# A two-block network on one core: two first units of a stage on the un-normed residual, the reciprocal norm on their result, and attention's first unit tile by tile

## The chip, the core and the metric

The kernel runs on one core of a Trainium2 chip. The metric is the device time of one execution in microseconds (us). Five engines run their own instruction streams and meet at semaphores: TensorE (PE, matmuls; PEld is its weight load), VectorE (DVE), ScalarE (ACT), GpSimd (POOL) and SyncE (SP), which starts the DMA transfers.

## The reference, cut to what matters

Two blocks of two layers work on `x`, 256 tokens by 1024 channels, in float32. Every layer is a feed-forward network, a mixer and a second network, and each of these stages begins with an RMS norm over the channels. In the first block:

```python
def rms_norm(x, g):
    xf = xf * lax.rsqrt(jnp.mean(xf * xf, axis=-1, keepdims=True) + NORM_EPS)
    return (xf * g).astype(x.dtype)

def swiglu_ffn(h, w_gu, w_down):
    gate, up = jnp.split(h @ w_gu, 2, axis=-1)
    return (jax.nn.silu(gate) * up) @ w_down

for layer in range(DEPTH):
    h = rms_norm(x, ffn1_norm[layer])
    x = x + 0.5 * swiglu_ffn(h, ffn1_w_gu[layer], ffn1_w_down[layer])
    h = rms_norm(x, mix_norm[layer])
    p = h @ w_in            # gates, an SGU branch, and a part that is shifted by one token
    ...                     # chunked SGU, RWKV-7 recurrence, projections
    x = x + merged @ w_out[layer]
    h = rms_norm(x, ffn2_norm[layer])
    x = x + 0.5 * swiglu_ffn(h, ffn2_w_gu[layer], ffn2_w_down[layer])
return rms_norm(x, final_norm)
```

In the second block the mixers are two attentions, and each norm is followed by a modulation with rows made from a condition vector: `h = rms_norm_2(x, g) * (1 + scale) + shift`, and the result of a stage enters `x` through a gate.

## The kernel before

**Layout.** Channels lie on the partitions: `x` is 8 tiles of 128 channels by 256 tokens, and so is the normed input `h_split`. Every product keeps float32 accuracy by splitting both operands into a rounded part and the rest and adding three matmuls (`three`, L1793 to L1795; `tokens_major` and the attention's helper have their own three, L2257 to L2259). Weights come from memory as 1 MB units of 16 tiles in three `raw_units` slots. A unit is two halves of 8 tiles. ACT writes the rounded part of a half (L852), DVE the rest (L1212), into four `split_halves` slots, and PE uses a pair of halves for one unit of two output tiles: 48 matmuls of 256 columns. Both engines are kept at most three halves ahead of PE by calls of `keep_ahead(w)` that stand at fixed places of their streams; a half can only be split when the slot's last user, four halves earlier, has been multiplied. Results go to three rotating PSUM banks, `linear_banks`.

**A network** (`ffn`) is 22 units for gate and up, each followed by SiLU on ACT (L915), the product on DVE (L1297) and the split of the result, and then a down stage of four pairs of output tiles (d = 0 to 3), each added to `x` by `residual` (L1316, L1323). During the networks DVE also works through the modulation matrix in dot products (L1278).

**A norm** (numbered 0 to 12 in program order; 6 closes the first block and 7 to 12 belong to the second) is a chain over three engines. ACT squares `x` two tiles at a time, PE sums the squares with a constant matrix in two float32 matmuls a pair (L1856, four records in the trace), ACT takes the root (L878) and DVE the reciprocal (L1227). Squares and sums of the pairs 0 to 2 are done in the stage before, as `x` becomes final; pair 3 can only follow the last residual. Then, in five steps (one tile, one tile, and three times two tiles), DVE multiplies `x` by gain and reciprocal (L1265, L1267), ACT rounds (L897; with the shift added L902) and DVE makes the rest (L1244; L1249 with shift). PE's first unit after a norm takes the tiles as they come (`h_wait`), its two halves turn by turn for each tile. In attention PE first waits for all eight tiles, then starts; the first unit of attention 0 has only 16 columns a matmul (the forget gates).

**What follows in the recurrent mixer** (`rwkv`): 13 units whose result ACT copies out of PSUM (L939, `raw_shift`), after which DVE forms the difference to the previous token (L1338) and mixes (L1347).

The order of all of this is written out by hand, engine by engine; `make_plan` only counts the uses of banks and halves.

## Time and profile before

| | |
|---|---|
| three runs, median | 3055.59 us (3054.66 to 3061.22) |
| the profiled execution, its own time | 3053.73 us |
| its span in the trace | 3052.0 us |
| PE busy | 2869.9 us, 94% |
| DVE busy | 1949.7 us, 64% |
| ACT busy | 1440.9 us, 47% |
| mean granted PE clock | 0.967 |

The profile lists each engine's busy time, the granted TensorE clock, the chain of work that ended last, and groups of instructions with what ended the idle time before them. Some 1.7 us lie outside the span. Matmuls overlap one another, so the number of matmuls started in a stretch says more than PE's busy share in it.

### The profile page before, as it was taken

The page shows a single profiled execution, that of the slowest core. Times are in us where ns is not written, and L with a number is a line of the kernel's source. Part 1 is how long each engine was busy: PE and PEld are TensorE (multiplying, and loading weights), DVE is VectorE, ACT ScalarE, POOL GpSimd, SP SyncE. Part 2 cuts the span into 40 slices and gives each one's busy share as a digit, 9 for nine tenths or more (in the row PEclk, how much of TensorE's full clock was granted, in tenths as well). Part 3 has the DMA queues.
Part 4 walks back from the last instruction along what each step waited for, and adds up shares of the span by engine and source line. Part 5 has one row for each costly group of instructions (what it writes and reads, how often), then busy time and mean ns, then how long its engine had stood idle before and what let it go on. Part 6 is the DMA issues. An engine that isn't in the chain of part 4 may idle for free.

```text
span 3052.0 us, 60529 instructions
## 1 busy us (share of the span) xinstructions
PE 2869.9 (94%) x26460; PEld 2738.7 (90%) x26460; DVE 1949.7 (64%) x2828; ACT 1440.9 (47%) x2121; POOL 13.2 (0%) x23
## 2 busy tenths in 40 slices
PE   7999989989999999899899899897999998998899
PEld 7999777889999997778899899886999998998899
DVE  5667556666666676566666666565666666776554
ACT  4445534344444445344344444464444445766443
POOL 0000000000000000000000000000000000000000
PEclk9999999999999999899999999898999999999899
DMA  6665311236656743111456566432665663342354
GB/s 228 238 247 180 111 43 43 84 138 235 248 196 252 264 161 118 50 44 43 166 192 234 182 236 243 161 125 83 239 244 196 252 250 131 133 150 100 129 188 140
DMA packets 72792, 511.09 MB, mean 167 GB/s; under 512 B 8464, under 2 KB 9104, under 8 KB 11728
## 3 DMA queue, kind: packets, MB, share of 16 engines
q1 hardware_dynamic: 72528, 507.21, 46.1%
q8 instruction: 209, 3.42, 0.4%
q14 instruction: 55, 0.45, 0.0%
HBM read 506.13 MB, written 1.05 MB: 166 GB/s over the span
## 4 chain that ended last, share of the span: by engine, by line
PE 89%; DVE 5%; ACT 4%; issue 1%; DMA 0%; SPq 0%; DVEq 0%; ACTq 0%
PE linear_banks L1793 22%; PE linear_banks L1794 21%; PE linear_banks L1795 21%; PE linear_banks L2257 3%; PE linear_banks L2258 3%; PE linear_banks L2259 3%; PE solve_banks L2123 1%; PE linear_banks L2089 1%; PE solve_banks L1856 1%; PE solve_banks L2132 1%; PE solve_banks L2220 1%; DVE rstd L1227 1%; PE solve_banks L2306 1%; PE solve_banks L2287 1%; PE solve_banks L2209 1%
## 5 line engine op out<-in xcount | busy, mean ns | idle before, releaser
L1212 DVE TENSOR_TENSOR split_halves<-raw_units,split_halves 128x1024 fp32r<-128x1024 f32 x806 | 981.5, 1223 | 580.4 <-ACT split_halves L852 578.5
L852 ACT ACTIVATE split_halves<-raw_units 128x1024 fp32r<-128x1024 f32 x806 | 846.3, 1056 | 672.6 <-PE linear_banks L1795 590.4
L1793 PE MATMUL linear_banks<-h_split,split_halves 128*128 128x256 f32 x3744 | 1088.0, 291 | 48.9 <-DVE h_split L1244 27.5
L1794 PE MATMUL linear_banks<-h_split,split_halves 128*128 128x256 f32 x3744 | 1071.5, 286 | 0.0
L1795 PE MATMUL linear_banks<-h_split,split_halves 128*128 128x256 f32 x3744 | 1070.9, 286 | 0.0
L1793 PEld LDWEIGHTS linear_banks<-h_split,split_halves 128*128 128x128 f32 x3744 | 730.6, 195 | 65.0 <-issue 50.5
L1794 PEld LDWEIGHTS linear_banks<-h_split,split_halves 128*128 128x128 f32 x3744 | 731.4, 195 | 2.0 <-issue 1.9
L1795 PEld LDWEIGHTS linear_banks<-h_split,split_halves 128*128 128x128 f32 x3744 | 730.8, 195 | 0.0
L1793 PE MATMUL linear_banks<-hidden_split,split_halves 128*128 128x256 f32 x1408 | 397.4, 282 | 0.0
L1795 PE MATMUL linear_banks<-hidden_split,split_halves 128*128 128x256 f32 x1408 | 394.7, 280 | 0.0
L1794 PE MATMUL linear_banks<-hidden_split,split_halves 128*128 128x256 f32 x1408 | 394.7, 280 | 0.0
L1794 PEld LDWEIGHTS linear_banks<-hidden_split,split_halves 128*128 128x128 f32 x1408 | 265.6, 189 | 0.4
L1793 PEld LDWEIGHTS linear_banks<-hidden_split,split_halves 128*128 128x128 f32 x1408 | 265.6, 189 | 0.4
L1795 PEld LDWEIGHTS linear_banks<-hidden_split,split_halves 128*128 128x128 f32 x1408 | 265.6, 189 | 0.0
L2257 PE MATMUL linear_banks<-split_halves,h_split 128*128 128x256 f32 (+1 forms) x784 | 229.8, 293 | 21.7 <-DVE h_split L1249 21.7
L2258 PE MATMUL linear_banks<-split_halves,h_split 128*128 128x256 f32 (+1 forms) x784 | 225.2, 287 | 0.0
L2259 PE MATMUL linear_banks<-split_halves,h_split 128*128 128x256 f32 (+1 forms) x784 | 224.9, 287 | 0.0
L915 ACT ACTIVATE silu<-linear_banks 128x256 f32<-128x256 f32 x176 | 67.6, 384 | 279.8 <-PE linear_banks L1795 279.7
L1278 DVE CUSTOM_DVE_ANT_0 raw_units<-raw_units,condition_rows,modulation 128x1024 f32<-128x1024 f32 x144 | 185.0, 1285 | 0.1
L2257 PEld LDWEIGHTS linear_banks<-split_halves,h_split 128*128 128x128 f32 x784 | 154.6, 197 | 26.1 <-DVE h_split L1249 22.4
L1297 DVE TENSOR_TENSOR gated<-silu,linear_banks 128x256 f32<-128x256 f32 x176 | 74.3, 422 | 151.6 <-ACT silu L915 148.2
L2258 PEld LDWEIGHTS linear_banks<-split_halves,h_split 128*128 128x128 f32 x784 | 154.8, 197 | 0.0
(291 smaller groups left out, 3397.0 us busy)
## 6 DMA issues: line engine op xcount, KB each, us to landing
raw_units<-in_stream SPq DMA_DIRECT2D x403, 1024.0 KB, 4.8
raw_units<-in_mod_w SPq DMA_DIRECT2D x72, 1024.0 KB, 6.4
x<-in_x SPq DMA_DIRECT2D x4, 256.0 KB, 5.1
w2a<-in_w2a SPq DMA_DIRECT2D x2, 512.0 KB, 6.2
w_rows<-in_w SPq DMA_DIRECT2D x2, 512.0 KB, 7.8
bs_rows<-in_bs SPq DMA_DIRECT2D x2, 512.0 KB, 8.7
spatial_t<-in_ws_t SPq DMA_DIRECT2D x2, 512.0 KB, 10.2
out<-x SPq DMA_DIRECT2D x4, 256.0 KB, 4.3
```

The costliest lines, as they stand in the source:

```text
L852: nc.scalar.activation(split[:, n % SPLIT_SLOTS, 0, :], raw[:, item % RAW_SLOTS, (n % 2) * HALF * P:(n % 2 + 1) * HALF * P], ACT.Copy).the ...
L915: nc.scalar.activation(silu[:, n % 3, :], bank[:, 0:T], ACT.Silu).then_inc(silu_ready, 1)
L1212: V.tensor_tensor(split[:, n % SPLIT_SLOTS, 1, :], raw[:, item % RAW_SLOTS, (n % 2) * HALF * P:(n % 2 + 1) * HALF * P], split[:, n % SPLIT ...
L1227: link(V.reciprocal(rstd[:], rstd[:]))
L1278: V.tensor_tensor_reduce(out=w, in0=w, in1=c_rows[:], scale=1.0, scalar=mod[:, n:n + 1], op0=ALU.mult, op1=ALU.add, accum_out=mod[:, n:n + ...
L1297: V.tensor_tensor(product[:, n % 3, :], silu[:, n % 3, :], bank[:, T:2 * T], ALU.mult)\
L1793: M(o, w_hi, a_hi, start=start, stop=False, skip_group_check=skip)
L1794: M(o, w_hi, a_lo, start=False, stop=False, skip_group_check=skip)
L1795: return M(o, w_lo, a_hi, start=False, stop=stop, skip_group_check=skip)
L2257: M(o, a_hi, s[:, 0, m], start=(c == 0 and j == 0), stop=False, skip_group_check=True)
L2258: M(o, a_lo, s[:, 0, m], start=False, stop=False, skip_group_check=True)
L2259: ins = M(o, a_hi, s[:, 1, m], start=False, stop=(c == DT - 1 and j == NCH - 1), skip_group_check=True)
```

## The change

For nine of the norms (`ROUGH`: 0 to 5, 9, 10 and 12) the first two units of the stage no longer wait for the norm. Since the reciprocal norm is one factor for each token, W(x·gain·r) = (W(x·gain))·r. So ACT and DVE split `x·gain` ("rough_split", eight tiles, rounded by `rough_high` and its rest by `rough_rest`), pairs 0 to 2 in the stage before and pair 3 right after the last residual; PE runs the two units on it (`first_tiles`, 96 matmuls in place of the same 96), and DVE multiplies the result by `rstd` on the way out of PSUM: into `first_units` for a network (`first_unit`), into `raw_shift` for the mixer, where it takes ACT's copy over for those two units. The sum of pair 3's squares now stands inside the first of these units, after 24 of its matmuls.

With a shift (norms 9, 10, 12) the shift vector is carried as two further columns of the moving operand (258 columns), written to PSUM banks of their own; its product is added as a bias in SiLU and in the product.

The normed `h_split` is still made in full, for unit 2 on. The splits of the halves 3, 4 and 5 of the new stage now stand inside the norm's chain on ACT and DVE, ahead of the root, ahead of step 2 and ahead of step 4.

In the two attentions (norms 8 and 11) PE waits in the first unit for each tile of `h_split` when it comes to it, with both token halves of a tile together. Norms 6 and 7 stay as they were.

```diff
+ROUGH = (0, 1, 2, 3, 4, 5, 9, 10, 12)
+EARLY_UNITS = 2
...
+    rough = over("rough_split", [P, 2, DT, T + 2], 44.25, F32R)
+    first = over("first_units", [P, EARLY_UNITS, 2, T], 68)
...
@@ ACT, norm
+                if n in ROUGH:
+                    if n:
+                        rough_high(n, 3)
+                    keep_ahead(first_half_of(n))
                 act.wait_ge(norm_summed, n + 1)
...
+            def rough_high(n, i):
...
+                for c in (2 * i, 2 * i + 1):
+                    ins = nc.scalar.activation(rough[:, 0, c, 0:T], x[:, c, :], ACT.Copy, scale=gain_of(n, c))
+                ins.then_inc(rough_hi, 1)
...
                 for s, tiles in enumerate(NORM_STEPS):
+                    if n in ROUGH and s in (2, 4):
+                        keep_ahead(first_half_of(n) + s // 2)
...
@@ DVE
+            def rough_rest(n, i):
...
+                for c in (2 * i, 2 * i + 1):
+                    ins = V.scalar_tensor_tensor(rough[:, 1, c, 0:T], x[:, c, :], gain_of(n, c),
+                                                 rough[:, 0, c, 0:T].bitcast(F32), ALU.mult, ALU.subtract)
+                ins.then_inc(rough_ready, 1)
...
+                if n in ROUGH:
+                    for i in range(3 if n else 0, 4):
+                        rough_rest(n, i)
+                    keep_ahead(first_half_of(n))
                 roots[0] += 1
                 root_wait()
...
+            def first_unit(i, j):
...
+                    V.tensor_tensor(first[:, j, :, :], pairs(bank), wide(rstd[:], 2), ALU.mult)\
+                        .then_inc(emptied["dve"], 1)
...
+                    if s < EARLY_UNITS:
+                        bank = wait_filled(dve, ("shift", l, s))
+                        V.tensor_tensor(raw_shift[:, n % 2, :, 1:T + 1], pairs(bank), wide(rstd[:], 2), ALU.mult)\
+                            .then_inc(emptied["dve"], 1)
...
@@ PE
+            def first_tiles(w, key, n, j):
...
+                for i, k in order:
+                    if j == 0 and i == 0:
+                        if n and k == 4:
+                            norm_sums(n, 3)
+                        pe.wait_ge(rough_ready, 4 * ROUGH.index(n) + k // 2 + 1)
...
@@ attention, PE
-                for k in range(DT):
-                    ready(k)
...
+                    if ready is not None and j == 0:
+                        ready(c)
```

**PE at norm 1** (end of the first network's down stage, start of the first recurrent mixer). `h_split` is the normed input, `hidden_split` the network's inner result, `solve_banks` here the bank of the norm's sum. Before:

```order
L1795 MATMUL linear_banks<-hidden_split,split_halves 128x256
L1856 MATMUL solve_banks<-squares,constants 128x256 [waits squared]
L1856 MATMUL solve_banks<-squares,constants 128x256
L1856 MATMUL solve_banks<-squares,constants 128x256 [waits squared]
L1856 MATMUL solve_banks<-squares,constants 128x256
L1793 MATMUL linear_banks<-h_split,split_halves 128x256 [waits lo_ready,h_ready,emptied_by_dve]
```

The same place now, its first rows, and then the rows around the second sum:

```order
L1907 MATMUL linear_banks<-hidden_split,split_halves 128x256
L1992 MATMUL solve_banks<-squares,constants 128x256 [waits squared]
L1992 MATMUL solve_banks<-squares,constants 128x256
L1905 MATMUL linear_banks<-rough_split,split_halves 128x256 [waits emptied_by_dve,rough_ready,lo_ready]
L1906 MATMUL linear_banks<-rough_split,split_halves 128x256
```

```order
L1907 MATMUL linear_banks<-rough_split,split_halves 128x256
L1992 MATMUL solve_banks<-squares,constants 128x256 [waits squared]
L1992 MATMUL solve_banks<-squares,constants 128x256
L1905 MATMUL linear_banks<-rough_split,split_halves 128x256 [waits rough_ready]
L1906 MATMUL linear_banks<-rough_split,split_halves 128x256
```

The sum of pair 3 moved behind 24 matmuls on `rough_split`, and the first wait for `h_ready` behind 96.

**DVE at norm 1**, from the residual of the last pair. Before, and then now; L1244 and L1330 write the rest of `h_split`, L1212 and L1275 the rest of a weight half:

```order
L1316 SCALAR_TENSOR_TENSOR x<-linear_banks,x 128x512 [waits lin_filled]
L1227 RECIPROCAL rstd<-rstd 128x256 [waits root_ready]
L1265 SCALAR_TENSOR_TENSOR squares<-x,columns,rstd 128x256 [waits dve_step]
```

```order
L1421 SCALAR_TENSOR_TENSOR x<-linear_banks,x 128x512 [waits lin_filled]
L1294 SCALAR_TENSOR_TENSOR rough_split<-x,columns,rough_split 128x256 [waits rough_hi,emptied_by_dve]
L1294 SCALAR_TENSOR_TENSOR rough_split<-x,columns,rough_split 128x256
L1275 TENSOR_TENSOR split_halves<-raw_units,split_halves 128x1024 [waits hi_ready]
L1311 RECIPROCAL rstd<-rstd 128x256 [waits root_ready]
L1348 SCALAR_TENSOR_TENSOR squares<-x,columns,rstd 128x256 [waits dve_step]
```

And the end of the chain, before and now:

```order
L1244 TENSOR_TENSOR h_split<-squares,h_split 128x512 [waits h_hi_ready] x2
L1330 MEMSET raw_shift 128x4
L1212 TENSOR_TENSOR split_halves<-raw_units,split_halves 128x1024 [waits hi_ready,dve_step]
L1212 TENSOR_TENSOR split_halves<-raw_units,split_halves 128x1024 [waits hi_ready]
L1338 TENSOR_TENSOR diff<-raw_shift 128x512 [waits emptied_by_act]
```

```order
L1330 TENSOR_TENSOR h_split<-squares,h_split 128x512 [waits h_hi_ready]
L1275 TENSOR_TENSOR split_halves<-raw_units,split_halves 128x1024 [waits hi_ready]
L1330 TENSOR_TENSOR h_split<-squares,h_split 128x512 [waits h_hi_ready]
L1435 MEMSET raw_shift 128x4
L1441 TENSOR_TENSOR raw_shift<-linear_banks,rstd 128x2x256 [waits lin_filled,dve_step]
L1447 TENSOR_TENSOR diff<-raw_shift 128x512 [waits emptied_by_dve]
```

The split of half 5 of the stage moved ahead of the last rest of `h_split`, and the product with `rstd` stands behind it.

## Rows read from the trace of the kernel before

**Rows 1.** The page's part 4: the chain that ended last, by engine.

```profile
PE 89%; DVE 5%; ACT 4%; issue 1%; DMA 0%; SPq 0%; DVEq 0%; ACTq 0%
```

**Rows 2.** Waits of PE: waiting line, whom for, us in total, times, longest.

```profile
PE linear_banks L1793 <- DVE h_split L1244: 27.5, 6, 8.1
PE linear_banks L2257 <- DVE h_split L1249: 21.7, 2, 11.6
```

**Rows 3.** Stretches: length, PE busy (matmuls), PEld, DVE, ACT, POOL, clock, DMA.

```profile
250.00:280.00 30.00, 30.00 (x252) 30.00 (x251) 20.88 (x28) 13.12 (x16) 0.00 (x0) 1.00 0.50 176
...
215.50:245.50 30.00, 25.55 (x195) 24.66 (x194) 22.34 (x33) 15.70 (x23) 0.00 (x0) 0.94 0.38 140
667.50:697.50 30.00, 25.55 (x187) 24.67 (x186) 21.04 (x31) 14.25 (x22) 0.00 (x0) 0.89 0.35 127
...
1066.00:1096.00 30.00, 25.55 (x184) 24.67 (x183) 21.10 (x32) 15.47 (x21) 0.00 (x0) 0.89 0.37 130
...
2116.00:2146.00 30.00, 25.14 (x187) 23.98 (x187) 22.35 (x39) 16.23 (x26) 0.00 (x0) 0.94 0.35 122
2315.70:2345.70 30.00, 25.14 (x181) 24.06 (x180) 21.61 (x36) 15.61 (x25) 0.00 (x0) 0.89 0.38 135
```

**Rows 4.** Timeline of PE at norm 1: start us, us, what, [idle before <- releaser].

```profile
217.01 1.02 PE L1856 MATMUL solve_banks<-squares,constants 128*128 128x256 f32 x4
218.61 1.13 PE L1856 MATMUL solve_banks<-squares,constants 128*128 128x256 f32 x4 [0.58 <-ACT squares L862]
223.62 0.55 PE L1793 MATMUL linear_banks<-h_split,split_halves 128*128 128x256 f32 x1 [3.87 <-DVE h_split L1244]
```

**Rows 5.** Timeline of ACT, then of DVE, at norm 1 and in unit 0.

```profile
219.78 0.47 ACT L878 ACTIVATE rstd<-solve_banks,constants 128x256 f32<-128x256 f32 x1 [1.22 <-PE solve_banks L1856]
222.59 0.81 ACT L897 ACTIVATE h_split<-squares 128x256 fp32r<-128x256 f32 x2 [2.34 <-DVE squares L1265]
...
220.29 1.75 DVE L1227 RECIPROCAL rstd<-rstd 128x256 f32<-128x256 f32 x1 [2.39 <-ACT rstd L878]
226.95 1.47 DVE L1244 TENSOR_TENSOR h_split<-squares,h_split 128x512 fp32r<-128x512 f32 x2
228.75 1.22 DVE L1212 TENSOR_TENSOR split_halves<-raw_units,split_halves 128x1024 fp32r<-128x1024 f32 x1 [0.31 <-ACT split_halves L852]
232.83 0.69 DVE L1338 TENSOR_TENSOR diff<-raw_shift 128x512 f32<-128x512 f32 x1
```

**Rows 6.** Timeline of DVE at norm 9, a norm with shift.

```profile
2120.68 1.75 DVE L1227 RECIPROCAL rstd<-rstd 128x256 f32<-128x256 f32 x1 [1.98 <-ACT rstd L878]
2127.74 0.88 DVE L1249 SCALAR_TENSOR_TENSOR h_split<-squares,modulation,h_split 128x256 fp32r<-128x256 f32 x2
```

**Rows 7.** PE idle in the first mixer and in its solve, and stretches behind such idle times.

```profile
358.56 0.39 PE L1793 MATMUL linear_banks<-h_split,split_halves 128*128 128x256 f32 x1 [2.39 <-ACT u L995]
...
407.80 0.27 PE L2132 MATMUL solve_banks<-z,inverse_blocks 64*64 64x64 f32 x1 [1.66 <-ACT z L1095]
...
359.60:362.60 3.00, 3.00 (x16) 3.00 (x15) 1.12 (x1) 0.00 (x0) 0.00 (x0) 0.50 0.28 55
...
407.00:411.00 4.00, 2.36 (x56) 1.94 (x58) 1.90 (x3) 1.49 (x4) 0.00 (x0) 1.00 0.44 186
```

**Rows 8.** Attention 0: first rest of `h_split`, PE's first unit. Attention 1: first and last rest, PE.

```profile
1948.54 0.49 DVE L1249 SCALAR_TENSOR_TENSOR h_split<-squares,modulation,h_split 128x256 fp32r<-128x256 f32 x1 [0.18 <-ACT h_split L902]
...
1955.20:1965.20 10.00, 10.00 (x48) 10.00 (x48) 2.25 (x2) 1.06 (x1) 0.00 (x0) 0.50 0.32 107
...
2523.61 0.66 DVE L1249 SCALAR_TENSOR_TENSOR h_split<-squares,modulation,h_split 128x256 fp32r<-128x256 f32 x1 [0.40 <-ACT h_split L902]
...
2529.89 1.22 DVE L1249 SCALAR_TENSOR_TENSOR h_split<-squares,modulation,h_split 128x256 fp32r<-128x256 f32 x2 [0.16 <-ACT h_split L902]
...
2531.50:2539.90 8.40, 8.33 (x48) 8.36 (x49) 4.97 (x17) 2.44 (x4) 0.00 (x0) 0.66 0.35 125
```

**Rows 9.** Timeline of ACT at the start of the program.

```profile
18.07 1.06 ACT L1183 ACTIVATE condition_rows<-condition_rows 128x1024 f32<-128x1024 f32 x1
```

More of the change, by code:

```diff
@@ L265, in make_plan @@
         for s in range(13):
[L266 removed]
+            p.use(("shift", l, s), "dve" if s < EARLY_UNITS else "act")
         for s in range(4):
@@ L739, in h_in, with gain_of, shift_row, first_half_of @@
         return t.rearrange("p (i r) -> p i r", r=4) if n == 11 else t
+    def gain_of(n, c):
+        if n >= 7:
+            return gain2[:, n - 7, c:c + 1]
+        l, w = divmod(n, 3)
+        return col(("ffn1_norm", "mix_norm", "ffn2_norm")[w], c, l)
+    def shift_row(n):
+        l, sub = divmod(n - 7, 3)
+        at_ = 72 * l + 24 * sub
+        return mod[:, at_:at_ + DT].unsqueeze(2).to_broadcast([P, DT, 2])
+    def first_half_of(n):
+        return MIX_AT[(1, 4, 8, 11).index(n)] if n in (1, 4, 8, 11) else FFN_AT[(0, 2, 3, 5, 7, 9, 10, 12).index(n)]
+    def gated(eng, i, j):
+        if j < EARLY_UNITS and ffn_norm(i) in ROUGH:
+            eng.wait_ge(first_gated, EARLY_UNITS * FIRST_OF[i] + j + 1)
+        else:
+            wait_emptied(eng, ("gu", i, j))
+    FIRST_OF = {i: n for n, i in enumerate(i for i in range(8) if ffn_norm(i) in ROUGH)}
     def x_wait(eng, n, i):
@@ L1182, in _ @@
             act.wait_ge(consts_loaded, 64)
+            for i in range(4):
+                rough_high(0, i)
             nc.scalar.activation(c_rows[:], c_rows[:], ACT.Silu).then_inc(c_ready, 1)
@@ L1292, in ffn @@
                     n = FT * i + j
+                    early = j < EARLY_UNITS and ffn_norm(i) in ROUGH
+                    if early:
+                        first_unit(i, j)
                     bank = wait_filled(dve, ("gu", i, j))
@@ L1845, in tokens_major @@
                 ins.then_inc(lin_filled, 1)
+            def first_tiles(w, key, n, j):
+                halves = [half_ready(w), half_ready(w + 1)]
+                if n >= 7:
+                    outs = [sv[:, 2 * j + i, 0:T + 2] for i in range(2)]
+                else:
+                    bank = bank_for(key)
+                    outs = [bank[:, i * T:(i + 1) * T] for i in range(2)]
+                order = [(i, k) for k in range(DT) for i in range(2)] if j == 0 else \
+                    [(i, k) for i in range(2) for k in range(DT)]
+                for i, k in order:
[3 more added lines that the diff above has]
+                        pe.wait_ge(rough_ready, 4 * ROUGH.index(n) + k // 2 + 1)
+                    s, o = halves[i], outs[i]
+                    t, m = slice(k * P, (k + 1) * P), o.shape[-1]
+                    ins = three(o, s[:, 0, t], s[:, 1, t], rough[:, 0, k, 0:m], rough[:, 1, k, 0:m],
+                                k == 0 and (n >= 7 or i == 0), k == DT - 1 and (n >= 7 or i == 1), skip=True)
+                    if k == DT - 1:
+                        ins.then_inc(halves_used if i == 0 else lin_filled, 1)
             def norm(n):
+                if n in ROUGH:
+                    return
                 for i in pairs_left(n):
```

118 lines of the change are left out of this document (85 added, 33 removed).

## The prediction

> **What bounds the kernel now.** Read the chain of waits first: 89% of it is PE [rows 1], so only PE's idle time and its slow stretches can be won. The list of waits then says where PE is idle: the longest entries are waits for `h_split`, that is for the norm's chain on DVE and ACT [rows 2]. Then measure the loss at each norm in matmuls, since a busy share hides it: 30 us without a norm hold 252 matmuls, 0.119 us each. The 30 us around norm 1 hold 195, those around norms 2 and 4 187 and 184, around norms 9 and 10 187 and 181 [rows 3]. (Norm 3 is like 1, 5 is the same as 4, 12 like 10, each within two.) The lost time is 30 - 0.119 x count: 6.8 us for norms 1 and 3, 7.7 for norm 2, 8.1 for 4 and 5, 7.7 for 9, 8.4 for 10 and 12. Sum of the first five 37.5, of the last three 24.5.
>
> What it consists of is seen at norm 1. The sums of pair 2 start at 217.01, right behind the down stage; those of pair 3 wait for the squares until 218.61; then PE stands still for 3.87 us and resumes at 223.62 [rows 4] with one tile of `h_split` at a time, at a clock that has partly fallen (0.94 or 0.89 of full speed over the 30 us [rows 3]).
>
> **The first two units on `rough_split`.** Four sum records stand at 0.217 us from one another (217.01 and 1.02 for four with the tail [rows 4]), so PE is free at 217.9. Now 24 rough matmuls follow, 2.9 us, to 220.8; their operands were split in the stage before. Then the sums of pair 3 (0.9 us), 72 more matmuls: 217.9 + 96 x 0.119 + 0.9 = 230.2. Pair 3 of `rough_split` needs ACT twice (0.81 us for two 256-column roundings) and DVE twice (0.88 us for a pair of such rests [rows 5, 6]) behind the squares; it is there by 220.5, PE needs it at 223.1. So PE runs without a gap through both units.
>
> What comes next is unit 2, and **it has a new last condition**. Its code asks for both its halves, 4 and 5, before its first tile, and half 5's rest now stands on DVE behind step 3 of the norm's chain. The chain itself starts later: the sums of pair 3 moved from 218.61 to 220.8, so the root goes from 219.78 to 221.9 and the reciprocal from 220.29 to 222.4, its end from 222.04 to 224.2 [rows 5]. From there to the end of step 3's rest was 5.65 us (227.7, the first of the two from 226.95 [rows 5]); with two half splits of 1.22 us in it that is 8.1 us, so unit 2 starts at 232.3. PE is idle for 2.1 us. The normed tiles of step 4 follow 0.7 us later and PE wants them 4.3 us later. Beside the idle time the eight sum records cost 0.8 us more than eight matmuls. What is left of a norm's loss is thus 2.9 us, at full clock.
>
> With a shift the stretch from the reciprocal's end (2122.43) to the same point (2128.62) is 6.2 us [rows 6], 0.55 more; and DVE's work after the chain (a bias copy, the product with `rstd`, SiLU, gating, a modulation dot, two rests) makes half 7 late by some 0.3 us. I take 3.6 us for norms 9, 10 and 12. The two extra columns are 2 of 258 and lie in 96 matmuls, under 0.1 us.
>
> Gain: 37.5 - 5 x 2.9 = 23.0, and 24.5 - 3 x 3.6 = 13.7. **Sum 36.7 us at full clock.**
>
> **What lies behind unit 2.** DVE owes two products with `rstd` (0.69 us each, as a 512-column difference [rows 5]) and the rest of units 0 and 1, and half 6 is queued behind the first of them. In the mixer: chain's end 0.7 us after unit 2's start, product, difference and two mixes 2.2, half 6's rest 1.2: 4.1 us after, PE needs it after 5.8. Half 7 comes at 7.7, needed at 8.6. In a network it is 0.1 us late at most. After that DVE needs about 4 of the 5.8 us of a unit and catches up. The PSUM bank of unit 0 is free 1.4 us after unit 2 starts, PE wants it after 5.8. No cost.
>
> **The rough pairs 0 to 2** lie in the down and out stages. In an out stage, a unit of 5.7 us, DVE has two rests (2.4), a residual (0.9) and now a pair (0.9): 4.2. ACT has two roundings, squares and 0.8: 3.6. Covered, with 1.5 us to spare on DVE; in a down stage, 15.7 us a pair of tiles, with far more. Cost 0; were the cover gone, each of 24 pairs (three at each of eight norms; norm 0 has none) would cost up to 0.9, 22 us.
>
> **The clock.** It is the unknown of the sum. After an idle time of 2.39 us PE went on at 358.56 and soon ran at half clock: 16 matmuls in 3.0 us from 359.6 at a granted clock of 0.50, the lower of its two levels (1.2 of 2.4 GHz) [rows 7], where full clock gives 25. How long a fall lasts is read from the 30 us around the norms: 0.94 of full speed is 3.6 us at half clock, 0.89 is 6.6 us [rows 3]. The short one costs half its length, 1.8 us, less what of it lies in idle time: I take 1.5. After an idle time of 1.66 us the clock stayed at 1.00 [rows 7]. The 2.1 to 2.6 us left at eight norms lie between the two, nearer to the first. I take six falls of 1.5 us: **-9.0**; the ends are none and eight falls of twice the length, 24.
>
> The Trainium skill (TensorE: Matmul & The Clock Gate, "Why this matters for your kernels") warns only of idle gaps longer than those left here. By it the sum would lose nothing to the clock; the 2.39 us row above speaks against it.
>
> **Attention's first unit.** Attention 0: PE's first unit began behind the last tile and took 10 us for 48 matmuls at a granted clock of 0.50 from 1955.2 [rows 8], ending at 1965.4. The first tile is there at 1949.0. Six matmuls a tile at 0.213 us are 1.28 us, about the pace at which the tiles come, so the unit ends at 1959.6 if the clock stays low: 5.8 us. Attention 1: first tile at 2524.3, last at 2531.1 [rows 8]. Before, PE starts behind it and has done the unit's 48 matmuls by 2539.9 [rows 8]. Now: at low clock throughout, paced by the tiles at first, about 11 us from 2524.3, end 2535.3, a gain of 4.6; at full clock it waits for the last tile and ends at 2531.1 + 1.4, a gain of 7.3. I take 6.0 and 5.5: **11.5**, ends 10.4 and 15.
>
> **Norm 0.** All eight tiles are made here, and DVE waits for the condition row first (`c_ready`), whose SiLU on ACT was at 18.07 for 1.06 us [rows 9] and moves behind eight roundings, 3.25 us, to 22.4. PE starts a little earlier than before, but the chain behind now has eight roundings (3.25 us) and eight rests (3.5 us) and two half splits (2.4 us) ahead of unit 2: 9.2 us, against two units of 5.7, which PE does meanwhile and which were stretched by the pace of the tiles before. With the chain's own 8.1 us and its later start the two come out about even. Between +2 and -2; I take a loss of 0.4.
>
> **Sum:** 36.7 - 9.0 + 11.5 - 0.4 = 38.8 us. The profiled execution took 3053.7 (its span and 1.7 us), so 3014.9. The median of the three runs stands 1.9 above it, within what runs differ by. I say **3015**.
>
> **The rivals.**
> *The clock stays up.* The waits of 2 us are too short to bring it down. For it: the 1.66 us row. Against: the 2.39 us row [rows 7]. Then 38.8 + 9.0 = 47.8, and attention 3 us nearer to its upper end: 3003.
> *More is left at each norm.* The clock falls every time and for twice as long (as around norms 2, 4 and 10 now, 0.89 [rows 3]), or one more half comes late. 24 instead of 9, perhaps 2 more: 3032.
> *Slower.* The rough pairs are not covered. An operation on `x` with a gain, rounded, has no row of its own; if a pair held up the next half so that PE lost more than 38.8 / 24 = 1.6 us at each of 24 places, the gain would be gone; with DVE's 1.5 us to spare that takes 4.0 us a pair instead of 0.9. At 2 us a place: 3053.7 - 38.8 + 48 = 3063. Against it: DVE is 20 to 22 us busy of 30 even around norms [rows 3].
> *It doesn't do what it says.* If a condition that I took as met long before (a bank, the gain of the next norm, half 3) releases `first_tiles` only when the old first tile came, only attention gains: 3042.
>
> **How the numbers follow.** Forecast 0.60, clock up 0.13, more left 0.20, only attention 0.04, slower 0.03. The range leaves out the last two and the far end of the third: 3001 to 3031. A measurement of this kernel can tell about 0.2%, 6 us, from no change. All cases but the slower one, and a tail of the fourth, are faster by more: faster 0.96, same 0.01, slower 0.03.
>
> **What would show it.** PE's first matmul on `rough_split` starts within 0.1 us of the end of pair 2's sums at eight norms, and 96 in a row at 0.12 us. One idle time of 2 to 2.6 us ahead of unit 2, released by `split_halves` on DVE, not by `h_split`. In the same 30 us around a norm 215 matmuls with a fall of the clock, (30 - 2.9 - 1.5) / 0.119, and 228 without. PE's waits for the rest of `h_split` near zero outside attention. A wait of PE in units 3 and 4, or in the down and out stages, would prove the covers wrong; a clock of 1.00 around the norms would prove the second case, one under 0.9 the third.

## The result and the profile after

| | before | changed |
|---|---|---|
| median of the runs | 3055.65 us (4 runs, 3054.66 to 3061.22) | 3006.04 us (4 runs, 3005.18 to 3013.84) |
| span of the profiled execution | 3052.0 us | 3005.0 us |
| PE, DVE, ACT busy | 2869.9, 1949.7, 1440.9 us | 2854.7, 1982.9, 1462.8 us |
| mean granted PE clock | 0.967 | 0.974 |

The ratio of the times is 0.984, with a 95% interval from 0.9819 to 0.986: the changed kernel is 1.6% faster. 3015 was forecast, so 9 us less than that was needed.

The page's parts 1 and 4 of the changed kernel. PE's share of the chain fell from 89% [rows 1] to 86%, and DVE's rose from 5% to 8%:

```profile
PE 2854.7 (95%) x26460; PEld 2726.5 (91%) x26460; DVE 1982.9 (66%) x2927; ACT 1462.8 (49%) x2192; POOL 13.9 (0%) x23
...
PE 86%; DVE 8%; ACT 4%; issue 2%; DMA 0%; SPq 0%; DVEq 0%; ACTq 0%
```

The list of waits (waiting line, whom for, us in total, times, longest). L1905 is `three` after the change, L2405 attention's helper, L1275 the rest of a weight half, L1330 and L1335 the rest of `h_split` without and with shift:

```profile
PE linear_banks L1905 <- DVE split_halves L1275: 19.5, 14, 2.5
...
PE linear_banks L2405 <- DVE h_split L1335: 8.9, 3, 4.5
...
PE linear_banks L1905 <- DVE rough_split L1294: 7.4, 1, 7.4
PE linear_banks L1905 <- DVE h_split L1335: 4.0, 1, 4.0
```

Both entries of [rows 2] have changed. The 27.5 us for `h_split` without shift are gone; a wait for a weight half stands there instead. The two waits of attention's first unit, 21.7 us, have become three of 8.9 together. The 7.4 us for `rough_split` is norm 0, the 4.0 norm 7, which was not changed.

**Norm 1 after the change.** This is the place of [rows 4] and [rows 5]; everything in it comes 1.0 us earlier in this execution (0.4 us of it already at PE's first matmul of the program, 0.6 at norm 0). First PE, then ACT, then DVE, each in order of start time (start us, us, what, [idle before <- releaser]):

```profile
215.99 1.02 PE L1992 MATMUL solve_banks<-squares,constants 128*128 128x256 f32 x4
216.67 0.47 PE L1905 MATMUL linear_banks<-rough_split,split_halves 128*128 128x256 f32 x1
...
219.72 1.03 PE L1992 MATMUL solve_banks<-squares,constants 128*128 128x256 f32 x4
...
229.03 0.28 PE L1907 MATMUL linear_banks<-rough_split,split_halves 128*128 128x256 f32 x1
231.05 0.36 PE L1905 MATMUL linear_banks<-h_split,split_halves 128*128 128x256 f32 x1 [1.74 <-DVE split_halves L1275]
```

```profile
217.45 0.90 ACT L941 ACTIVATE rough_split<-x,columns 128x256 fp32r<-128x256 f32 x2
...
220.79 0.47 ACT L919 ACTIVATE rstd<-solve_banks,constants 128x256 f32<-128x256 f32 x1 [1.49 <-PE solve_banks L1992]
```

```profile
218.45 0.88 DVE L1294 SCALAR_TENSOR_TENSOR rough_split<-x,columns,rough_split 128x256 fp32r<-128x256 f32 x2 [1.57 <-ACT rough_split L941]
...
221.29 1.75 DVE L1311 RECIPROCAL rstd<-rstd 128x256 f32<-128x256 f32 x1 [0.73 <-ACT rstd L919]
...
229.57 1.22 DVE L1275 TENSOR_TENSOR split_halves<-raw_units,split_halves 128x1024 fp32r<-128x1024 f32 x1
230.71 0.68 DVE L1330 TENSOR_TENSOR h_split<-squares,h_split 128x512 fp32r<-128x512 f32 x1
231.45 0.69 DVE L1441 TENSOR_TENSOR raw_shift<-linear_banks,rstd 128x512 f32<-128x512 f32 x1
```

PE goes from the sums of pair 2 straight into `rough_split` (216.67), takes the sums of pair 3 after 24 matmuls (219.72), and stops once, for 1.74 us, ahead of unit 2 (231.05). The releaser is DVE's split at 229.57, half 5, queued behind the chain's step 3.

**Around the eight norms.** The same 30 us as in [rows 3], each beginning at the same matmul of PE as there, for norms 1, 2, 3, 4, 5, 9, 10, 12 in this order. The columns: length, PE busy (matmuls), PEld, DVE, ACT, POOL, clock, DMA share, GB/s:

```profile
214.60:244.60 30.00, 28.26 (x231) 27.87 (x230) 26.60 (x40) 17.45 (x24) 0.00 (x0) 1.00 0.44 154
662.50:692.50 30.00, 27.70 (x224) 27.10 (x223) 24.78 (x38) 15.46 (x26) 0.00 (x0) 1.00 0.36 128
857.70:887.70 30.00, 27.71 (x224) 27.11 (x223) 24.01 (x36) 15.56 (x24) 0.00 (x0) 1.00 0.38 140
1053.00:1083.00 30.00, 28.27 (x231) 27.88 (x230) 26.73 (x42) 18.20 (x25) 0.00 (x0) 1.00 0.47 157
1511.20:1541.20 30.00, 27.69 (x224) 27.10 (x223) 24.64 (x38) 15.30 (x26) 0.00 (x0) 1.00 0.36 126
2087.30:2117.30 30.00, 27.70 (x213) 27.31 (x212) 25.14 (x47) 17.63 (x30) 0.00 (x0) 0.94 0.32 113
2283.90:2313.90 30.00, 26.58 (x214) 25.99 (x213) 24.38 (x45) 16.19 (x27) 0.00 (x0) 1.00 0.35 126
2806.70:2836.70 30.00, 27.20 (x219) 26.62 (x218) 24.56 (x42) 19.22 (x33) 0.00 (x0) 1.00 0.37 127
```

Together 1780 matmuls in 240 us; at 0.119 us each that is 28.2 us lost, against the 62.0 of the prediction's first paragraph: a gain of 33.8. The clock column is the news: it was 0.94 or 0.89 in all of [rows 3] that hold a norm, and is 1.00 around seven of eight.

**Attention.** DVE's first tile of attention 0; PE's start there and in attention 1; and the stretches of the 48 matmuls behind these two starts:

```profile
1924.24 0.48 DVE L1335 SCALAR_TENSOR_TENSOR h_split<-squares,modulation,h_split 128x256 fp32r<-128x256 f32 x1 [0.18 <-ACT h_split L957]
```

```profile
1924.87 0.35 PE L2405 MATMUL linear_banks<-split_halves,h_split 128*128 128x16 f32 x1 [4.03 <-DVE h_split L1335]
...
2488.57 0.55 PE L2405 MATMUL linear_banks<-split_halves,h_split 128*128 128x256 f32 x1 [4.49 <-DVE h_split L1335]
```

```profile
1924.80:1935.30 10.50, 10.33 (x48) 10.26 (x48) 7.97 (x16) 4.72 (x8) 0.00 (x0) 0.50 0.21 69
2488.50:2497.40 8.90, 8.40 (x48) 8.13 (x49) 8.35 (x24) 5.24 (x8) 0.00 (x0) 0.67 0.01 2
```

PE starts 0.15 us after the first tile's rest and does the unit while the other tiles come, at the lower clock, as forecast. PE runs its 26460 matmuls in the same order in both kernels but for the moved sums, so one and the same matmul can be looked up in both traces. From 60 matmuls ahead of the first unit to 300 behind its start, attention 0 took 61.8 us before and 56.5 now, attention 1 59.1 and 52.5: a gain of 12.0.

**Where the 47.0 us of span went:** 33.8 at eight norms by the counts, 12.0 in attention, 0.6 at norm 0 (from PE's first matmul to 300 behind the first unit's start, 51.9 and 51.3 us); the other 0.6 is within the rounding of eight counts.

Measured with these stretches of 360 matmuls, the eight norms took 409.8 us before and 375.4 now, 34.4 less, and with that nothing is left over. This sum, called the eight stretches below, is what the experiments are compared by: it leaves out the rest of the program, whose clock differs from execution to execution (last section).

### The profile page after: what moved, and what is told of

It is laid out like the page before. It is cut to its first block, busy times and chain, and to the rows that moved or that the text cites. A ratio compares the mean times of both kernels' runs of the same rounds, so it can differ in the third digit from the quotient of the medians.

```text
span 3005.0 us, 60748 instructions
## 1 busy us (share of the span) xinstructions
PE 2854.7 (95%) x26460; PEld 2726.5 (91%) x26460; DVE 1982.9 (66%) x2927; ACT 1462.8 (49%) x2192; POOL 13.9 (0%) x23
## 4 chain that ended last, share of the span: by engine, by line
PE 86%; DVE 8%; ACT 4%; issue 2%; DMA 0%; SPq 0%; DVEq 0%; ACTq 0%
PE linear_banks L1905 21%; PE linear_banks L1906 20%; PE linear_banks L1907 20%; PE linear_banks L2405 3%; PE linear_banks L2406 3%; PE linear_banks L2407 3%; DVE split_halves L1275 2%; PE solve_banks L2268 1%; PE solve_banks L1992 1%; PE linear_banks L2234 1%; PE solve_banks L2277 1%; DVE squares L1348 1%; PE solve_banks L2364 1%; DVE rstd L1311 1%; PE solve_banks L2454 1%
## 5 line engine op out<-in xcount | busy, mean ns | idle before, releaser
L1275 DVE TENSOR_TENSOR split_halves<-raw_units,split_halves 128x1024 fp32r<-128x1024 f32 x806 | 980.5, 1223 | 514.3 <-ACT split_halves L889 512.5
L1905 PE MATMUL linear_banks<-h_split,split_halves 128*128 128x256 f32 x3456 | 998.2, 289 | 28.6 <-DVE split_halves L1275 19.5
L1906 PE MATMUL linear_banks<-h_split,split_halves 128*128 128x256 f32 x3456 | 982.7, 284 | 0.0
L1907 PE MATMUL linear_banks<-h_split,split_halves 128*128 128x256 f32 x3456 | 982.3, 284 | 0.0
L1905 PEld LDWEIGHTS linear_banks<-h_split,split_halves 128*128 128x128 f32 x3456 | 667.5, 193 | 42.9 <-issue 24.7
L1906 PEld LDWEIGHTS linear_banks<-h_split,split_halves 128*128 128x128 f32 x3456 | 668.1, 193 | 2.0 <-issue 1.9
L1907 PEld LDWEIGHTS linear_banks<-h_split,split_halves 128*128 128x128 f32 x3456 | 667.9, 193 | 0.0
L1905 PE MATMUL linear_banks<-hidden_split,split_halves 128*128 128x256 f32 x1408 | 397.3, 282 | 0.0
L1905 PEld LDWEIGHTS linear_banks<-hidden_split,split_halves 128*128 128x128 f32 x1408 | 265.6, 189 | 0.4
L2405 PE MATMUL linear_banks<-split_halves,h_split 128*128 128x256 f32 (+1 forms) x784 | 230.1, 294 | 9.0 <-DVE h_split L1335 8.9
L2405 PEld LDWEIGHTS linear_banks<-split_halves,h_split 128*128 128x128 f32 x784 | 154.5, 197 | 13.9 <-issue 10.9
L2406 PEld LDWEIGHTS linear_banks<-split_halves,h_split 128*128 128x128 f32 x784 | 154.9, 198 | 0.0
L2407 PEld LDWEIGHTS linear_banks<-split_halves,h_split 128*128 128x128 f32 x784 | 154.6, 197 | 0.0
```

The source lines that it names most:

```text
L1275: V.tensor_tensor(split[:, n % SPLIT_SLOTS, 1, :], raw[:, item % RAW_SLOTS, (n % 2) * HALF * P:(n % 2 + 1) * HALF * P], split[:, n % SPLIT ...
L1905: M(o, w_hi, a_hi, start=start, stop=False, skip_group_check=skip)
L1906: M(o, w_hi, a_lo, start=False, stop=False, skip_group_check=skip)
L1907: return M(o, w_lo, a_hi, start=False, stop=stop, skip_group_check=skip)
L2405: M(o, a_hi, s[:, 0, m], start=(c == 0 and j == 0), stop=False, skip_group_check=True)
L2406: M(o, a_lo, s[:, 0, m], start=False, stop=False, skip_group_check=True)
```

## The experiments

The theory: PE's idle time ahead of unit 2 and, in networks and at norms with shift, the wait for half 7 are what is left of a norm's loss; the clock mostly stays up because the idle time is short enough. A first rival: attention or norm 0 carries part of the gain ascribed to the eight norms. A second: the clock came up for a reason that has nothing to do with the idle time.

### One part alone

The kernel before with the change of attention only: `ROUGH = ()`, ACT copies all 13 units of the mixer out of PSUM, and no unit is taken from `rough_split`.

```diff
-ROUGH = (0, 1, 2, 3, 4, 5, 9, 10, 12)
+ROUGH = ()
```

> The kernel before with the attention part of the change alone (tile-by-tile first unit at norms 8 and 11; no norm handled early). Theory 'the parts add': matched matmul by matmul, the traces of before and after differ by 4.4 us over attention 0's first units and by 6.7 us over attention 1's, so 3055.7 - 11.1 = 3044.5 us. Rival 'the parts help each other' (half of the attention gain is an earlier clock that only the early units bring): under 6 us of gain, 3050 us or more.

Measured 3042.39 us (3040.94 to 3044.2) against 3055.91 before, ratio 0.9955 (0.9939 to 0.9972). The eight stretches are 410.2, as before; the two of attention 109.0, as in the changed kernel, against 121.0 before.

The changed kernel without the attention part:

```diff
                 ready = h_wait(8 + 3 * l)
+                for k in range(DT):
+                    ready(k)
...
-                                    ready if n < 2 else None)
+                                    None)
```

> The changed kernel with attention's first unit as before (PE waits for all eight normed tiles at norms 8 and 11). Theory 'the parts add': 3006.0 + 11.1 = 3017 us, and 37 to 39 us gained by the early units against before. Rival 'they help each other': 3011 us or less, or over 3022.

Measured 3022.64 us (3017.62 to 3028.35), ratio 0.9893 (0.9878 to 0.9908). The eight stretches are 376.7, attention's two 120.2 against 121.0 before. Alone, the parts gain 13.5 and 33.3 us, together 46.8; the changed kernel has 49.6 by the medians of its first comparison and 46.9 in a later one. They add up, and neither hides behind the other. This kernel came out 5 us slower than expected; its trace is slower in the first recurrence, which ran at a lower clock and has its section at the end.

### Norm 0 as before

```diff
-ROUGH = (0, 1, 2, 3, 4, 5, 9, 10, 12)
+ROUGH = (1, 2, 3, 4, 5, 9, 10, 12)
```

> The changed kernel with norm 0 handled as in the kernel before (PE's first two units on the normed tiles). The prediction had a loss of 0.4 us for norm 0's part, the trace shows the matmuls of the first network 1.0 us earlier. Theory 'norm 0 gives nothing that can be measured': 3006 to 3007 us; rival 'a gain of some us': over 3010 us.

Measured 3007.49 us (3005.17 to 3012.74), ratio 0.9846 (0.9832 to 0.9861). The stretch of norm 0 took 52.07 us, against 51.3 in the changed kernel and 51.9 before, the eight stretches 375.3. What norm 0 gives is under 1 us and can't be told from nothing by the runs, nor by the traces: in the five other traces that handle norm 0 and its halves as the changed kernel does, the stretch took 51.5 to 52.3 us, so the 0.6 us above isn't shown to be a gain. The rival of norm 0 falls.

### The idle time made longer

One more product on DVE, 0.69 us by its own row and 0.73 in PE's idle time, into a buffer that nobody reads, ahead of half 5 in the chain of the eight norms. It lengthens PE's idle time and puts off DVE's work behind it by as much; nothing else is changed.

```diff
                 for s, tiles in enumerate(NORM_STEPS):
+                    if n in ROUGH and n and s == 4:
+                        for _ in range(1):
+                            link(V.tensor_tensor(squares_copy[:], x[:, 0:2, :], x[:, 0:2, :], ALU.mult))
                     if n in ROUGH and s in (2, 4):
                         keep_ahead(first_half_of(n) + s // 2)
```

> The changed kernel with one more DVE instruction of 0.7 us (a product of x with itself, thrown away) ahead of the split of half 5 in the norm's chain at eight norms: PE's idle time ahead of unit 2 grows from 1.74 to about 2.5 us at norms 1 to 5 and from 2.3 to 3.0 at norms 9, 10 and 12. Theory 'length of the idle time decides the clock': falls at norms 1 to 5 too, 8 x 0.73 + 6 or 7 x 1.5 = 15 to 16 us more, 3021 us, granted clock under 1.00 in the 30 us around most norms. Rival 'an idle time beside dense matmuls on both sides does not bring the clock down': 5.8 us more, 3012 us, clock 1.00 around norms 1 to 5.

Measured 3025.72 us (3016.95 to 3026.68), ratio 0.9896 (0.9881 to 0.9911). PE's restart at norm 1, and four of the eight stretches, norms 1, 2, 9 and 10:

```profile
233.25 0.36 PE L1909 MATMUL linear_banks<-h_split,split_halves 128*128 128x256 f32 x1 [2.47 <-DVE split_halves L1276]
```

```profile
216.10:246.10 30.00, 27.53 (x213) 27.14 (x212) 25.79 (x39) 15.88 (x22) 0.00 (x0) 0.94 0.41 141
674.10:704.10 30.00, 27.52 (x212) 27.13 (x211) 24.75 (x39) 15.51 (x26) 0.00 (x0) 0.94 0.34 118
...
2103.70:2133.70 30.00, 26.97 (x207) 26.59 (x206) 25.11 (x47) 17.58 (x30) 0.00 (x0) 0.94 0.31 106
2301.00:2331.00 30.00, 26.97 (x208) 26.59 (x207) 24.35 (x45) 16.16 (x27) 0.00 (x0) 0.94 0.34 118
```

The clock is 0.94 in all eight stretches, where the changed kernel has 1.00 in seven. So 0.73 us more of idle time did bring the clock down: the second rival falls, and with it the idea that a wait of two to three microseconds can't do this.

The price of a fall is read from the counts. At norm 1, 231 matmuls became 213, which is 18 x 0.119 = 2.1 us, of which 0.73 is the added operation: the fall cost 1.4. At norm 2, 224 became 212, 1.4 us, the fall 0.7. At norm 10, 214 became 208, 0.7 us, the fall nothing. The three differ by the wait for half 7, which DVE makes at its own pace: the changed kernel has none at norm 1, 0.55 us at norm 2 and 1.12 at norm 10:

```profile
688.43 0.39 PE L1905 MATMUL linear_banks<-h_split,split_halves 128*128 128x256 f32 x1 [0.55 <-DVE split_halves L1275]
...
2310.47 0.39 PE L1905 MATMUL linear_banks<-h_split,split_halves 128*128 128x256 f32 x1 [1.12 <-DVE split_halves L1275]
```

A slower PE comes later to half 7 and waits less for it. With the operation added these two waits are gone. Norm 12 has no wait for half 7 to give back, and there the stretch grew from 47.5 to 49.2 us, 1.0 of it for the fall. The eight stretches took 387.1 us, 11.7 more: 5.8 for the operations and 5.9 for the clock.

With two such operations (`range(2)`), so an idle time of 3.2 us, and 3.8 to 4.0 with shift:

> The same with two such instructions: idle times of about 3.2 and 3.8 us. Theory 'length decides': a fall at every one of the eight norms, 11.7 + 8 x 1.5 = 23.7 us more, 3030 us, and more where it lasts twice as long. Rival 'dense matmuls keep it up': 11.7 us more, 3018 us, clock 1.00.

Measured 3029.6 us (3025.9 to 3031.3), ratio 0.9913 (0.9899 to 0.9928); the eight stretches 394.8, which is 19.4 more than the changed kernel: 11.7 for the operations, 7.7 for the clock. It fell at seven of the eight norms, at three of them for 6.8 instead of 3.4 us, and at norm 4 not at all.

### The idle time taken away

Halves 4 and 5 both at step 2 of the chain:

```diff
-                    if n in ROUGH and s in (2, 4):
-                        keep_ahead(first_half_of(n) + s // 2)
+                    if n in ROUGH and s == 2:
+                        keep_ahead(first_half_of(n) + 2)
```

> The changed kernel with the splits of the halves 4 and 5 both ahead of step 2 of the norm's chain, on ACT and DVE (half 5 one step and 2.8 us earlier). Tests that half 5's rest is what releases unit 2. Theory 'unit 2 waits for half 5, and DVE's queue behind the chain is the next bound': PE's idle time ahead of unit 2 goes from 1.74 to 0 at norms 1 to 5, but DVE does the same work by the same time, so in networks half 7 still comes at the old time and PE stands still for about 2 us ahead of it instead of 0.55; only the two mixers keep their 1.4 us. 3006.0 - 3 = 3003 us. Rival 'the idle time is all there is to win': 5 x 1.74 + 3 x 2.3 = 15.6 us less, 2990 us.

Measured 3009.19 us (3007.84 to 3011.89), ratio 0.9851 (0.9836 to 0.9865), no different from the changed kernel; the 3 us that were expected can't be seen in the total, and in this trace the first recurrence took 8 us longer than in the changed kernel's. In the trace PE has no idle time ahead of unit 2 at any of the eight norms; at norms 9, 10 and 12 it waits 2.3 to 2.6 us for half 6 instead. At norms 1 and 4 that is won (240 matmuls instead of 231), at norm 2 it comes back in unit 3, once for half 6 and once for half 7:

```profile
691.11 0.36 PE L1905 MATMUL linear_banks<-h_split,split_halves 128*128 128x256 f32 x1 [1.27 <-DVE split_halves L1275]
695.43 0.38 PE L1905 MATMUL linear_banks<-h_split,split_halves 128*128 128x256 f32 x1 [1.21 <-DVE split_halves L1275]
```

```profile
215.00:245.00 30.00, 29.62 (x240) 29.03 (x239) 26.74 (x41) 17.32 (x24) 0.00 (x0) 1.00 0.45 151
669.40:699.40 30.00, 27.52 (x222) 26.93 (x222) 24.69 (x38) 15.40 (x26) 0.00 (x0) 1.00 0.34 124
```

1.27 + 1.21 is 2.5 us, where the changed kernel has 1.75 + 0.55 = 2.3. By these rows, in a network DVE's total work from the reciprocal to half 7 is what binds; its order only chooses where PE waits for it. The eight stretches took 374.3 us, 1.1 less than in the changed kernel.

The sum of pair 3 after 12 matmuls instead of 24, which starts the chain earlier:

```diff
-                        if n and k == 4:
+                        if n and k == 2:
                             norm_sums(n, 3)
```

> The changed kernel with pair 3's squares summed after 12 of the first unit's matmuls instead of 24. The root could start 1.4 us earlier, but DVE still has pair 3's rests and half 3 ahead of the reciprocal, which leaves 0.73 us. Theory 'the chain's start moves everything behind it': idle time ahead of unit 2 1.0 instead of 1.74 us at norms 1 to 5 and 1.6 instead of 2.3 at the others, and half 7 earlier by the same: 8 x 0.73 = 5.8 us less, 3000 us. Rival 'the sums cost at their new place, since the squares are not ready': 3006 us.

Measured 3007.64 us (3005.89 to 3008.06), ratio 0.9843 (0.9826 to 0.9859). The eight stretches took 373.3 us, 2.1 less, not the 5.8 that was hoped for. At norm 3 the idle time ahead of unit 2 is 0.90 us instead of 1.74, at norm 2 it is 1.37, and PE's wait for half 7 stays at 0.54 us in both. The clock fell at norm 12, whose stretch took 48.5 us instead of 47.5: that is 1.0 us of what is missing.

### Less on DVE behind the norm

If DVE's work up to half 7 binds, taking some of it away should win what reordering could not. First try: both edits above, and the networks' modulation dot products (1.28 us each on DVE) moved one unit later.

```diff
-MOD_SPREAD = ((0,), (1,), ())
+MOD_SPREAD = ((), (0,), (1,))
```

> Both of these changes, and the modulation's first dot product of every network one unit later (unit 2 instead of 1), so that DVE reaches half 7 1.2 us earlier. Theory 'DVE's queue behind the chain is the bound once half 5 is early': no idle time ahead of unit 2 and under 0.5 us ahead of half 7; 1.75 us less at each of the two mixers, about 1.9 at norms 2, 3 and 5, 2.0 at norms 9 and 10, 0.7 to 1.5 at norm 12: 14 to 15 us less, 2991 us, and the granted clock 1.00 around the eight norms. Rival 'the rest of the gain needs PE, ACT or DMA': not under 2998 us.

Measured 3045.95 us (9 runs, 3041.52 to 3052.97), ratio 0.9971 (0.9961 to 0.9981): nearly all of the change's gain was gone. Around the norms the expectation held in part only. There is no idle time ahead of unit 2, half 7 is late by 0.4 to 0.6 us, and the clock did not fall; but half 6 was now late, by 0.4 to 0.9 us at norms 2, 3 and 5 and by 1.6 to 2.0 with shift, and at five of the eight a wait of 1.3 to 1.4 us follows at the start of unit 6. The eight stretches took 374.6 us, 0.8 less than in the changed kernel, where 14 to 15 were expected. The 40 us of loss lie in the rest of the networks. A stretch in the middle of one, in the changed kernel and then in this one, and the waits of this kernel:

```profile
700.00:730.00 30.00, 30.00 (x252) 30.00 (x252) 21.22 (x30) 14.28 (x21) 0.00 (x0) 1.00 0.73 267
```

```profile
700.00:730.00 30.00, 27.66 (x227) 27.13 (x226) 16.70 (x24) 10.87 (x17) 0.00 (x0) 1.00 0.65 248
```

```profile
PE linear_banks L1905 <- DVE split_halves L1275: 46.3, 53, 2.7
...
ACT split_halves L889 <- DMA raw_units<-in_stream: 472.0, 132, 8.9
```

In the changed kernel the last entry reads 98.7 us in 40 waits. That the moved dot products are the cause is shown by the last of the eight networks, in which none runs. From 300 to 1500 matmuls behind the first unit's start, the other seven took 1008.0 us together in the changed kernel and 1048.4 here, 40.4 more; the last took 142.8 in both. How they do it is read from the code: the modulation matrix passes through the same three `raw_units` slots as the weights, so a dot product also frees a slot. One unit later, the next weight unit is asked for one unit later, and ACT stands waiting for it 132 times. DVE was relieved where it was short by delaying what the stream of weights hangs on.

Second try: the dot products stay in their units, only half 7's split is drawn ahead of the dot product of unit 1; again with both edits above.

```diff
+                    if j == 1 and ffn_norm(i) in ROUGH:
+                        keep_ahead(base + 2 * j + 2)
                     if i < MOD_NETWORKS and 0 < j <= 3 * MOD_FFN:
```

> The changed kernel with the halves 4 and 5 split ahead of step 2, pair 3 summed after 12 matmuls, and half 7's split ahead of the modulation's first dot product in unit 1 (the dot stays in that unit, so the stream's slots come free as before, 1.2 us later once a network). Theory 'DVE's queue behind the chain bounds the eight norms, and moving the dot a whole unit failed only through the stream': no wait for the stream's DMA beyond those of the changed kernel, idle time ahead of unit 2 near 0 at norms 1 to 5, half 7 late by under 0.3 us at norms 2, 3 and 5. Against the changed kernel's stretches around the eight norms (375.4 us in sum): 1.5 us less at norms 1 and 4, 1.9 at 2, 3 and 5, 1.5 at 9, 10 and 12, 13 us less in all, 362 us, and 2993 us for the kernel, give or take 5 us that the clock in the recurrences adds or takes. Rival 'the stream is at its limit around the networks' starts': waits for DMA of over 20 us and no gain.

Measured **2997.67 us** (2993.73 to 3002.8), ratio 0.9809 (0.9795 to 0.9824). The changed kernel itself ran again beside it:

> The changed kernel itself, on the same chip in the same rounds. 3006 us if its first measurement was typical; the granted clock in the first recurrence decides over some 8 us (428 us against 420 us for the same instructions), so up to 3014 us in single runs.

Measured 3009.64 us (3006.78 to 3014.35), ratio 0.9852 (0.9836 to 0.9869). So the version with the three edits is 12 us faster than the changed kernel in the same rounds, with no overlap of their runs. Its stretches of norms 2, 4 and 12:

```profile
664.60:694.60 30.00, 28.66 (x232) 28.06 (x231) 24.29 (x38) 15.54 (x27) 0.00 (x0) 1.00 0.34 128
...
1053.30:1083.30 30.00, 29.82 (x243) 29.41 (x243) 27.92 (x43) 17.96 (x26) 0.00 (x0) 1.00 0.45 159
...
2796.60:2826.60 30.00, 27.11 (x217) 26.31 (x216) 24.05 (x41) 18.81 (x33) 0.00 (x0) 1.00 0.34 126
```

The counts are 232, 243 and 217, where the changed kernel has 224, 231 and 219: networks and mixers gained, norm 12 did not. PE waits only once in the middle of the networks (1008.6 us by the measure above), though ACT's waits for the stream grew from 98.7 to 171.2 us, which the expectation had excluded. All eight sum to 1838, 58 more than in the changed kernel, 6.9 us. The eight stretches took 368.3 us, 7.1 less than in the changed kernel's first trace, where the expectation had 362: at norm 2 PE still waits 0.90 us for half 6 and 0.44 for half 7, and at norms 9 and 12 2.0 us for half 6. With the run of the changed kernel beside it, whose eight stretches took 377.5, the difference is 9.2 of the 9.9 us by which the spans of the two traces differ; 1.2 are in attention's two stretches, which took 107.6 and 108.8. Of the 9.2, some 2.3 are from norms 4 and 10, where only the changed kernel's clock fell and its idle time at norm 4 was 0.7 us longer. Alone, the first edit took 1.1 us off the eight stretches and the second 2.1; the third was not run without them, so its own share of the 7.1 isn't known.

## Why the prediction was right, point by point

**The first two units.** Right: PE's first matmul on `rough_split` starts 0.68 us after the first of pair 2's sums (0.87 was worked out), that is right behind the four, and 96 matmuls follow with only the sums of pair 3 between them. The reciprocal starts at 221.29, forecast 222.4 less the 1.0 us by which the place is earlier. The cover of the rough pairs held: PE waits for `rough_split` only at norm 0.

**The new last condition.** Right in kind and nearly in size: one idle time ahead of unit 2, released by half 5's rest and not by `h_split`. It was forecast at 2.1 us and is 1.74 at norms 1 to 5, and 2.3 to 2.5 at norms 9, 10 and 12 (forecast 2.6).

**Half 7** was sized too low. It was to be late by 0.1 us in networks and 0.3 with shift. It is late by 0.55 and, at norm 10, by 1.12. That is most of why the loss at norm 2 is 30 - 0.119 x 224 = 3.3 us and at norm 10 4.5, instead of 2.9 and 3.6 (with shift the prediction's own terms, 2.9 + 0.55 + 0.3, give 3.75, and it took 3.6). The eight norms together lose 28.2 us, forecast 25.3 at full clock: 2.9 more, with the one fall of the clock in it.

**The clock** is the term that was mis-sized. Six falls of 1.5 us were taken off, 9.0. There was one fall, at norm 9, and it cost 0.1 us: the stretch of 360 matmuls took 48.25 us, and 48.14 in the second trace of the changed kernel, where the clock stayed up at norm 9. Two steps failed there. The chance of a fall was read off one row at 2.39 us of idle time [rows 7], and 1.74 us turned out to be on the safe side mostly. And the price assumed that a slower PE is late for everything behind it; the longer idle times showed that at norms 2, 3, 5, 9 and 10 the wait for half 7 pays back half of it or all. A fall cost 1.3 to 1.5 us at norms 1 and 4, where PE waits for nobody behind unit 2, and 1.0 at norm 12. The other traces with unchanged DVE work agree: norm 10 with a fall 47.78, without 47.67 us; norms 2 and 5 with one 47.7, without 47.0; norm 4 with one 47.87, without 45.69, of which 0.7 is a longer idle time ahead of unit 2.

**Attention** was forecast at 6.0 + 5.5 = 11.5 us and gained 5.4 + 6.6 = 12.0. Attention 1 did better than taken, since the clock was not low throughout the unit, as one end of the estimate had it (0.67 over the stretch).

**Norm 0** was taken at a loss of 0.4 and was 0.6 quicker in the trace; both are too small to be told from nothing.

**The sum.** 27.7 was forecast for the eight norms with the clock in it, and 33.8 came: 6.1 of the 8 us by which the span was shorter than forecast. The 6.1 are 8.9 for the clock, less 2.8 for the larger loss at the norms. So the result lies between the forecast and its rival "the clock stays up" (3003), nearer to the latter. A clock of 1.00 around the norms was the prediction's own sign for that rival, and seven of eight norms show it: of the two cases it is the one with a chance of 0.13 that came, and the time is as near to 3015 as it is because the norms lost 2.8 us more than worked out, mostly for half 7. That the two errors partly cancel was luck. The forecast of 215 matmuls with a fall and 228 without was good for norm 1 (231 without; 213 with the added operation, which itself is worth 6, so 219 with a fall alone). "More is left at each norm" is excluded by the stretches, "only attention gains" by the first experiment, and "slower" by the absent waits in the down and out stages.

## What to carry to other kernels

Where a factor commutes with a product, let the product run on what is there and multiply afterwards: the chain that makes the factor then has the product's time as cover. What is left of the loss moves to the next thing queued behind that chain on the helping engine, so list that engine's work up to the second and third thing PE will ask for, not only the first; here reordering it moved the wait, and drawing one split ahead of a dot product won 12 us together with two earlier splits and an earlier sum. Before an operation is delayed to relieve an engine, look at which buffer it frees and who fills that buffer next.

## What the runs showed of the hardware

**Idle time and the clock.** The longest idle time of PE in units 2 and 3 behind each of the eight norms, and whether the granted clock was at its lower level of 1.2 instead of 2.4 GHz at or within 2 us of the restart, in the traces of the changed kernel (twice) and of the eight variants that keep its early units. The other 6 of the 80 places have no idle time over 0.3 us there and no fall:

| idle time, us | places | with a fall |
|---|---|---|
| 0.4 to 1.67 | 17 | 0 |
| 1.74 to 1.78 | 19 | 2 |
| 2.02 to 2.06 | 6 | 1 |
| 2.26 to 2.33 | 10 | 5 |
| 2.42 to 2.48 | 6 | 6 |
| 2.52 to 2.55, all at norm 12 | 5 | 0 |
| 3.03 and more | 11 | 10 |

One of the six in the row of 2.42 to 2.48 is norm 4 of the changed kernel's second trace (2.42 us), where the other traces with DVE's order unchanged have 1.74. Ahead of that norm ACT had waited 5.0 us for a unit of the weight stream, against 3.1 in the first trace, and the norm's chain ran late: the idle time itself depends on when a transfer lands. So there is no sharp limit. The same kernel at the same place falls in one execution and not in the next: at norm 9 with 2.31 us in the changed kernel's first trace, not with 2.33 in its second, where norm 10 fell instead. Norm 12 doesn't fit the row above it, and nothing here says why; that it has to do with what PE did earlier is a guess. The Trainium skill (TensorE: Matmul & The Clock Gate, "Why this matters for your kernels") warns only of gaps longer than those of all rows but the last; the 2.46 to 2.48 us of idle time at norms 1 to 5, with a fall at each, differ from that, and the measurement decides.

**The same work at another clock.** The first recurrence, about 4745 matmuls that no edit here touches, took 420.0 us in the kernel before. In the changed kernel, then with attention's part alone, then with the early units alone:

```profile
234.70:655.10 420.40, 389.34 (x4746) 345.93 (x4745) 273.42 (x475) 186.11 (x297) 4.88 (x8) 0.97 0.27 97
```

```profile
240.30:664.10 423.80, 392.97 (x4746) 348.24 (x4745) 270.14 (x468) 184.67 (x294) 4.88 (x8) 0.96 0.27 96
```

```profile
235.50:663.60 428.10, 397.20 (x4746) 350.99 (x4745) 273.32 (x475) 186.46 (x297) 4.88 (x8) 0.95 0.27 95
```

Over all twelve traces the stretch took 417.3 to 428.8 us, of which 17 to 44 us were at the lower level of the clock; the shortest had the least of it, the longest the most. The total follows the clock as well, since every run has its mean granted clock on record: in the nine runs of the kernel with the moved dot products it goes from 0.975 to 0.971 as the time goes from 3041.5 to 3053.0 us. By an estimate from these numbers, 0.004 of 3045 us is 12 us, and the times differ by 11.5, the largest spread of one kernel here. What makes the clock fall oftener in one execution of a kernel than in another isn't shown. It does mean that a variant is better judged by the stretches that its edit touches than by one total. The 5 us by which the early units alone missed their expectation are less than what this stretch differs by (428.1 against 420.4). In the version with the three edits and in the changed kernel beside it the stretch took the same, 423.9 and 423.7 us, so it has no part in their difference.
